# Turns of the RWKV operands placed behind the attention units, and a reordered HGRN2 head on TensorE

## The reference

```
# attention: p = softmax(q.k/8 + c_t - c_s, causal), o = p.v
# RWKV-7:
S = S * w_t + (S a_t) b_t^T + v_t k_t^T
y_t = S r_t
# then group norm of y, plus bonus (sum of r*k*r_k) * v, times a gate
```

```
f = lb + (1 - lb) * sigmoid(f_logit);  k = 1 - f;  b = cumsum(log f) within a chunk
a   = einsum('td,sd,tsd->ts', q, k, exp(b_t - b_s), causal)
o   = a @ v + (q * exp(b)) @ state
state = exp(b_last) * state + (k * exp(b_last - b))^T @ v
# o is divided by its root mean square and multiplied by a weight and silu(gate)
```

## Time and profile before

| | us |
|---|---|
| median of three runs (3396.19 to 3407.8) | 3400.59 |
| the profiled execution | 3394.34 |
| its span | 3392.6 |
| TensorE busy (97%) | 3306.0 |
| VectorE busy (57%) | 1931.4 |
| ScalarE busy (37%) | 1254.7 |

### The profile page before, as it was taken

How to read it: one execution, slowest core, us unless ns; L and a number is a source line. 1 busy time by engine, 2 the same in 40 slices (tenths; PEclk the granted TensorE clock), 3 DMA queues, 4 the chain that set the end, 5 groups by cost and what they waited for, 6 DMA issues and landing times.

```text
span 3392.6 us, 50022 instructions
## 1 busy us (share of the span) xinstructions
PE 3306.0 (97%) x18459; PEld 2704.5 (80%) x18459; DVE 1931.4 (57%) x3749; ACT 1254.7 (37%) x1622; POOL 132.2 (4%) x54
## 2 busy tenths in 40 slices
PE   8998999999899999999999999999999999999998
PEld 6665877878577788888878887888888888888886
DVE  5455456552565544452355999998885444444443
ACT  3333233322455433342343334444544333333332
POOL 0000000000000000000001545000000000000000
PEclk9987999999999999999999999999999999999999
DMA  4110012323222222222332444455556655555542
GB/s 145 56 38 1 4 51 81 99 93 100 86 65 67 80 76 79 80 74 93 100 106 79 148 141 143 156 180 182 185 177 220 228 198 192 198 194 196 198 142 81
DMA packets 145995, 408.03 MB, mean 120 GB/s; under 512 B 11225, under 2 KB 43993, under 8 KB 143585
## 3 DMA queue, kind: packets, MB, share of 16 engines
q1 hardware_dynamic: 73520, 265.85, 25.7%
q10 hardware_dynamic: 72368, 140.68, 11.5%
HBM read 337.28 MB, written 69.21 MB: 120 GB/s over the span
## 4 chain that ended last, share of the span: by engine, by line
PE 87%; DVE 10%; ACT 1%; issue 1%; DMA 1%; ACTq 0%; DVEq 0%; SPq 0%
PE bank L337 24%; PE bank L339 24%; PE bank L338 24%; PE bank L959 2%; PE bank L445 2%; PE bank L957 2%; PE bank L889 1%; ACT arena L1000 1%; PE bank L464 1%; DVE arena L2057 1%; PE bank L503 1%; DVE arena L2020 1%; DVE arena L2021 1%; DVE arena L2023 1%; PE bank L372 1%
## 5 line engine op out<-in xcount | busy, mean ns | idle before, releaser
L337 PE MATMUL bank<-xs,ring_hi 128*128 128x512 f32 x2488 | 990.9, 398 | 19.9 <-DVE xs L1564 9.7
L339 PE MATMUL bank<-xs,ring_lo 128*128 128x512 f32 x2488 | 971.8, 391 | 0.0
L338 PE MATMUL bank<-xs,ring_hi 128*128 128x512 f32 x2488 | 971.3, 390 | 0.0
L1000 ACT ACTIVATE arena<-bank 128x512 f32<-128x512 f32 (+4 forms) x584 | 392.1, 706 | 1013.1 <-PE bank L339 726.8
L1000 ACT ACTIVATE ring_hi<-ring 128x1024 fp32r<-128x1024 f32 x503 | 532.4, 1061 | 621.4 <-DMA ring<-weights 425.3
L1557 DVE TENSOR_TENSOR ring_lo<-ring,ring_hi 128x1024 fp32r<-128x1024 f32 x246 | 300.2, 1224 | 519.5 <-ACT ring_hi L1000 484.0
L337 PEld LDWEIGHTS bank<-xs,ring_hi 128*128 128x128 f32 x2488 | 468.8, 188 | 127.9 <-issue 14.4
L339 PEld LDWEIGHTS bank<-xs,ring_lo 128*128 128x128 f32 x2488 | 468.3, 188 | 100.9
L338 PEld LDWEIGHTS bank<-xs,ring_hi 128*128 128x128 f32 x2488 | 469.2, 189 | 97.1 <-issue 3.4
L2070 DVE TENSOR_TENSOR ring_lo<-ring,ring_hi 128x1024 fp32r<-128x1024 f32 x206 | 252.6, 1226 | 387.3 <-ACT ring_hi L1000 387.2
L337 PE MATMUL bank<-gw,ring_hi 128*128 128x512 f32 x1024 | 398.5, 389 | 0.7 <-ACT arena L1000 0.7
(11 more groups left out here) (285 smaller groups left out, 3408.4 us busy)
## 6 DMA issues: line engine op xcount, KB each, us to landing
ring<-weights SPq DMA_DIRECT2D x503, 512.0 KB, 3.6
hidden<-arena ACTq DMA_DIRECT2D x128, 256.0 KB, 4.1
gates<-arena ACTq DMA_DIRECT2D x16, 2048.0 KB, 6.6
arena<-hidden ACTq DMA_DIRECT2D x16, 2048.0 KB, 10.3
arena<-gates ACTq DMA_DIRECT2D x16, 2048.0 KB, 16.9
xres<-x_t ACTq DMA_DIRECT2D x4, 512.0 KB, 6.5
out_t<-arena SPq DMA_DIRECT2D x4, 512.0 KB, 3.0
arena<-ret_decay ACTq DMA_DIRECT2D x1, 1024.0 KB, 5.9
```

Source lines behind the costliest of these rows:

```text
L337: pe.matmul(out_, wh, x[0], start=start, stop=False, skip_group_check=True)
L338: pe.matmul(out_, wh, x[1], start=False, stop=False, skip_group_check=True)
L339: return pe.matmul(out_, wl, x[0], start=False, stop=stop, skip_group_check=True)
L1000: return act.activation(out_, in_, f, **kw)
```

## The change

**RWKV turns.** The six turns of TA and TB leave `rw_prepare`, with ScalarE's copies and the two semaphores. The late stage now turns TA, TB, TK and RV of all four pairs, sixteen turns in that order. All counts of `rw_act` and `rw_pe` behind it grow by 6.

**HGRN2 head.** The turned keys wait for a semaphore of their own, `hg_keys`, given after KD. The products by chunk stand in front of the scores. The outputs are issued from inside the fourth dense block, in front of its last chunk. ScalarE's square stands in front of Silu. VectorE's mask of the scores waits for the fourth step of `hg_pe` and the state chain for the third.

```diff
-                if u in (19, 20, 23, 24, 27, 28):
-                    i, g0 = (u - 19) % 4, (u - 19) // 4
-                    pe.wait_ge(rw_dve, 2 * g0 + 2)
-                    if 2 * g0 + i:
-                        pe.wait_ge(tok_out, 2 * g0 + i)
-                    for g in range(TT):
-                        tr = pe.transpose(bank[1][:, g * P:(g + 1) * P], tile((TA, TB)[i] + g0)[:, g * P:(g + 1) * P], cc("ident"))
-                    tr.then_inc(tok_ready, 1)
                 if u in (17, 21, 25, 29):
                     pe.wait_ge(rw_dve, 2 * m + 1)
-                    if m:
-                        pe.wait_ge(tok_out, 2 * m)
...
             pe.wait_ge(rw_dve, 8)
-            pe.wait_ge(tok_out, 2 * (NPAIR - 1))
-            late = [(TA, 3), (TB, 3)] + [(TK, m) for m in range(NPAIR)] + [(RV, m) for m in range(NPAIR)]
-            for j, (src, m) in enumerate(late):
+            for i, (src, _) in enumerate(((TA, MA), (TB, MB), (TK, MK), (RV, MV))):
+                for m in range(NPAIR):
+                    j = 4 * i + m
...
                     if r == 0:
-                        pe.wait_ge(rw_act, 30)
+                        pe.wait_ge(rw_act, 36)
...
-                pe.wait_ge(hg_dve, h * 6 + 4)
+                pe.wait_ge(hg_keys, h + 1)
                 for g in range(TT):
                     tr = pe.transpose(bank[5][:, g * P:(g + 1) * P], tile(H_["KD"])[:, g * P:(g + 1) * P], cc("ident"))
                 tr.then_inc(hg_pe, 1)
-                for g in range(TT):
-                    cols = slice(g * P, (g + 1) * P)
-                    mm = pe.matmul(bank[6][:, cols], tile(H_["KD"])[:, cols], tile(H_["QD"])[:, cols],
-                                   start=True, stop=True, skip_group_check=True)
-                mm.then_inc(hg_pe, 1)
                 pe.wait_ge(hg_act, h * 6 + 4)
...
-                product(q + 3, [(B_HG + 3, KD)], XS, h, 4, 4)
-                pe.wait_ge(hg_dve, h * 6 + 6)
+                pe.wait_ge(hg_dve, h * 6 + 4)
...
+                def outputs(k):
+
+                    if k != KD - 1:
+                        return
+                    pe.wait_ge(hg_dve, h * 6 + 6)
...
+                product(q + 3, [(B_HG + 3, KD)], XS, h, 4, 4, outputs)
...
-                if u in (20, 21, 24, 25, 28, 29):
-                    i, g0 = (u - 20) % 4, (u - 20) // 4
-                    act.wait_ge(tok_ready, 2 * g0 + i + 1)
-                    A(tile((MA, MB)[i] + g0), bank[1][:, :], ACT.Copy).then_inc(tok_out, 1)
...
+                act.wait_ge(hg_pe, h * 6 + 5)
+                A(tile(H_["SQ"]), bank[7][:, :], ACT.Square).then_inc(hg_act, 1)
                 act.wait_ge(block_used, h * 4 + B_HG + 4)
-
                 act.wait_ge(hg_dve, h * 6 + 1)
                 A(tile(H_["G"]), bank[(q + 3) % NBANK][:, :], ACT.Silu).then_inc(evac, 1)
                 dense(B_HG + 6, h, 4)
-                act.wait_ge(hg_pe, h * 6 + 5)
-                A(tile(H_["SQ"]), bank[7][:, :], ACT.Square).then_inc(hg_act, 1)
...
-                st.go(TTN(tile(H_["KD"]), tile(H_["K"]), tile(H_["EM"]), ALU.mult))
+                TTN(tile(H_["KD"]), tile(H_["K"]), tile(H_["EM"]), ALU.mult).then_inc(hg_keys, 1)
...
+                ve.wait_ge(hg_pe, h * 6 + 4)
+                TTN(v4(tile(H_["AM"])), v4(bank[6][:, :]), mask4("incl_T"), ALU.mult).then_inc(hg_dve, 1)
                 ve.wait_ge(hg_pe, h * 6 + 3)
-                TTN(v4(tile(H_["AM"])), v4(bank[6][:, :]), mask4("incl_T"), ALU.mult).then_inc(hg_dve, 1)
-                ve.wait_ge(hg_pe, h * 6 + 4)
```

More of the change, by code:

```diff
@@ L826, in _ @@
                 mm.then_inc(hg_pe, 1)
[L827 to L828 removed]
+                pe.wait_ge(hg_dve, h * 6 + 4)
                 for g in range(TT):
                     cols = slice(g * P, (g + 1) * P)
[L831 to L837 removed]
+                    mm = pe.matmul(bank[6][:, cols], tile(H_["KD"])[:, cols], tile(H_["QD"])[:, cols],
+                                   start=True, stop=True, skip_group_check=True)
+                mm.then_inc(hg_pe, 1)
+                def outputs(k):
+                    if k != KD - 1:
+                        return
+                    pe.wait_ge(hg_dve, h * 6 + 6)
+                    for g in range(TT):
+                        cols = slice(g * P, (g + 1) * P)
+                        pe.matmul(bank[7][:, cols], v4(tile(H_["IT"]))[:, g, :], tile(H_["AM"])[:, cols],
+                                  start=True, stop=False, skip_group_check=True)
+                        for c in (2 * g, 2 * g + 1):
+                            if c:
+                                mm = pe.matmul(bank[7][:, c * C:(c + 1) * C], H_["S"](c), tile(H_["QD"])[:, c * C:(c + 1) * C],
+                                               start=False, stop=(c % 2 == 1), skip_group_check=True)
+                    mm.then_inc(hg_pe, 1)
+                product(q + 3, [(B_HG + 3, KD)], XS, h, 4, 4, outputs)
                 pe.wait_ge(hg_act, h * 6 + 5)
@@ L1140, in _ @@
             pair_copy(NPAIR - 1)
-            late = [(MA, 3), (MB, 3)] + [(MK, m) for m in range(NPAIR)] + [(MV, m) for m in range(NPAIR)]
-            for j, (dst, m) in enumerate(late):
-                act.wait_ge(rw_pe, 20 + j + 1)
-                A(tile(dst + m), bank[j % 2][:, :], ACT.Copy).then_inc(rw_act, 1)
+            for i, dst in enumerate((MA, MB, MK, MV)):
+                for m in range(NPAIR):
+                    act.wait_ge(rw_pe, 20 + 4 * i + m + 1)
+                    A(tile(dst + m), bank[(4 * i + m) % 2][:, :], ACT.Copy).then_inc(rw_act, 1)
             for r in range(2):
-                pb = 30 + RW_PE * r
+                pb = 36 + RW_PE * r
                 for lev in range(5):
@@ L1165, in _ @@
                 A(XS[k][0], tile(OF + k), ACT.Copy).then_inc(hi_ready, 1)
-            bp = 30 + RW_PE * 2 + 22
-            ba = 30 + RW_ACT * 2
+            bp = 36 + RW_PE * 2 + 22
+            ba = 36 + RW_ACT * 2
             for m in range(NPAIR):
```

28 lines of the change are left out of this document (11 added, 17 removed).

## The result

| | before | after |
|---|---|---|
| median of 7 runs | 3396.19 us (3391.18 to 3410.45) | 3366.29 us (3362.43 to 3383.43) |
| profiled execution | 3394.34 us | 3383.43 us |
| mean granted clock of it | 0.984 | 0.985 |

The ratio is 0.992 (95% interval 0.9895 to 0.9945). The medians lie 30 us apart, where 15.6 were forecast.

What follows compares the result with a forecast made beforehand. TensorE was taken as the bound (87% of the last-ending chain). From 3394.3 us, 9.5 for the loop and 6.2 for eight heads left 3378.6; with the median 6.2 above the profiled run, 3385 us, range 3371 to 3399.

Steps and rivals of the forecast that it cites:

- part 1: Attention loop: six turn groups move behind it; 11.2 us removed, 4.2 added, 7.0 at the old clock, 9.5 taken.
- The sign that was to decide: Granted clock from 250 to 300 us: 0.65 to 0.8 for the forecast, over 0.9 for the first rival.
- The bonus product's wait for VectorE: Attention loop: wait for VectorE's first step of the pair, costed at nothing; shows if TensorE outruns VectorE by a unit.
- the clock term: Attention loop: clock effect of removed waits, between 11 us lost and 18.5 gained for part 1; 9.5 gained taken.
- The upper end: Attention loop at full clock, bounded by VectorE: 66.7 us become 44, 22.7 less, 18.5 net of late groups.
- the third rival: Clock wakes later without the dense transposes: part 1 loses its gain, heads give 6, median about 3396; chance 0.10.
- Part 2: Recurrence head: chunk products before scores, key transposes waiting only for decayed keys; gain 0.2 us a head.
- Part 3: Recurrence head: outputs ahead of the fourth block's last chunk, sum of squares at T + 8.3; gain 0.57 us a head.
- The clock stays up: Attention loop mostly at 2.4 GHz, VectorE the bound: part 1 gives 15 to 18 us, median 3377; chance 0.27.
- Outputs wait for the state chain: Recurrence heads: part 3 gains nothing, parts 1 and 2 together 9 us, median 3391; chance 0.13.
- The slower case: Late stage and first chunk products at low clock: 27 us more, less 6, median 3422; chance 0.05.
- The base: Whole kernel: median before taken as 3400.59 us, 6.2 us above the profiled execution, added to the sum.

Runs made afterwards that it cites:

- e12: The changed kernel once more, unchanged: 3364.46 us, ratio 0.9923; its profile is nearer the median.
- e1: Kernel before with only the six RWKV turns moved behind the loop, heads unchanged: 3375.15 us, ratio 0.9929.
- e3: Kernel before, all turns left in the loop, ScalarE copying each turned tile one unit earlier in its queue: 3368.33 us, ratio 0.9914.
- e5: Changed kernel plus eight matmuls of 128 x 512 without use in unit 13: 3367.25 us, ratio 0.9918.
- e7: e3's edit (turns in the loop, earlier copies) with the recurrence heads of the changed kernel: 3361.15 us, ratio 0.9899.
- e8: e9 with the eight matmuls of e5 added: 3358.32 us, ratio 0.9888.
- e9: e7 with head turns moved into the third block, scores into the fourth, state chain ahead of the mask: 3352.26 us, ratio 0.9881.
- e6: Kernel before plus the same eight matmuls without use in unit 13: 3395.44 us, ratio 0.9998.
- e10: Kernel before with ScalarE copying both tiles where it copied the first, so only the turn of TB waits: 3385.19 us, ratio 0.9983.
- e11: Kernel before with the first copy a unit earlier, the second unchanged, so only the bonus product waits: 3385.69 us, ratio 0.9987.
- e4: e1 with TensorE still waiting at the old places for ScalarE copies of the same size, without use: 3398.55 us, ratio 1.0012.
- e2: Kernel before with only the recurrence head's reordering, turns unchanged: 3386.73 us, ratio 0.9972.

## Why the prediction was right or wrong, point by point

**The steps that held.** The waits behind VectorE's decayed queries, ahead of the sum of squares, and behind ScalarE's copies in the loop left as said. Sixteen late groups took 11.25 us for the 11.4 forecast; the first stood at 303.94 us in the profile after, for 304 forecast. That agreement is luck: the execution profiled was the slowest of seven, with a low stretch that reached to 271 us. In it part 1 gives 324.93 - 315.19 = 9.7 us, the forecast term. In e12 it gives 324.93 - 298.35 = 26.6 us. The sign that was to decide, the clock from 250 to 300 us, would have misled in the same way. It reads 0.79 in the profile after, inside the forecast's 0.65 to 0.8, but through one fall that began before 250 us and not through falls as before; in e12 it reads 1.00. The bonus product's wait for VectorE, costed at nothing, came: three times in e12, 1.5 us in all.

**The step that failed** is the choice of the clock term: 9.5 us, "nearer to 7.0, since the clock was just as low where TensorE had no wait (215 to 250 us...)". Part 1 alone measured 19 us by the medians and 24 by the ratio (17 to 32, e1). The row was right and the inference was not. It shows how long one fall lasts, with TensorE busy all the while; it says nothing about what starts the next ones. The kernel before falls once near 221 us without a wait, as every kernel here does, and then three times within 3 us of a wait behind a copy. I weighed the first as evidence against the others. The right question was: if these waits go, which fall has a reason left? None behind 250 us, as e3, e5, e7, e8, e9 and e12 show.

The arithmetic of it, from the earlier trace rows and the e12 rows: from 215 to 311 us the kernel before spent 24 us (0.66 over 35) and 41 us (0.66 over 61) at 1.2 GHz, some 65 us; e12 spent 10 (0.85 over 35). Work that runs at half speed for 55 us less saves up to 27 us. From its own side: the way to the first late turn is 317.71 - 287.10 = 30.6 us shorter, and six groups at 0.68 us (4.0) come back behind it.

**The upper end** of that term was too low too, 18.5 against 26.6 us. Reckoning VectorE as the next limit was right, as its 33.68 busy of 35 us show. But I began at 250.98 us, and of the 7.9 us by which the way to the first late turn shrank beyond my 22.7, 4.0 came earlier (bonus product at 239.30 for 243.32), because how long the first low stretch lasts varies; 1.2 came behind the last bonus product (8.5 us before, 7.3 in e12), a part that I had held fixed; the other 2.7 lie between.

**The Trainium skill** ("TensorE: Matmul & The Clock Gate", section on what is actually happening), with its "the default state is throttled, and activity releases the throttle", was weighed both ways in the prediction. Its good side came true: idleness out, clock up. Its bad side, that the dense transposes were needed, didn't behind 271 us: e1, e5 and e12 have none of the six groups in the loop and stay at 1.00 behind the first stretch. For the first stretch itself it stays open (see the third rival). The eight added matmuls of e5 and e6, more activity in the plainest sense, changed nothing; in these runs it was the missing idleness that counted.

**The heads.** Forecast 0.77 us a head, measured 0.63 (30.30 to 29.67), so 5.0 instead of 6.2 us. Part 2 gave 0.30 for 0.2. Part 3 gave 0.34 for 0.57: the outputs came at T + 5.18 instead of T + 5.05, since the chain ended at T + 5.12, and outputs and the last three matmuls took 3.35 us, not 3.25. ScalarE's slack of 3.37 us fell to 0.52, for 0.6 reckoned, and nothing of its later root reached TensorE. The drain that the Trainium skill ("ScalarE: Activation LUTs", section on what a table load costs) puts beside each load didn't show again: the load at 1026.49 took 1.28 us, and the next instruction started at 1027.78.

**The rivals.** "The clock stays up", given 0.27, was the right mechanism; its 17 us for part 1 stand against 19 to 24 in e1 and 26.6 in the rows of e12, so its median of 3377 us was 11 us too slow as well. "Outputs wait for the state chain" came to some 0.3 us a head, not 0.57. The clock did not stand low in the chunk products. That it wakes later is neither shown nor excluded. In e12 it didn't (up at 233 us, 1.00 from there on). But in the profiles of the five kernels without the six groups in the loop the first low stretch ended at 233, 236, 245, 267 (e1) and 271 us (after), and in those of the nine kernels with them between 231 and 249. No run tests whether the groups end it; if they do, it is one more reason why e3 (3368.33) is faster than e1 (3375.15) by more than the 4 us of late groups. The slower case was not seen in any run.

**The base.** 3400.59 us was the median of three runs. In the 7, 23, 17 and 23 runs beside the result and the experiments it was 3396.19, 3394.41, 3393.91 and 3391.19 us. With a base of 3396 my sum would have read 3380.5, still 14 us too slow; the base is not the reason for the miss, but 4 of the 19 us between 3385 and 3366.29 are its. The range moved with it would have begun at 3366.6, right at the measured median; that closeness would have been luck, since the clock term was wrong all the same.

**What stays open:** why the clock falls near 220 us, where TensorE is busy without a gap, and what decides whether that stretch lasts 10 us (e3, e12), 24 (before), 48 (e1) or 51 (the profile after). Between the two profiles of the changed kernel it makes 17 of 19 us (first chunk product at 315.19 and 298.35 us, executions of 3383.43 and 3364.43 us), and by the mean clocks most of the spread from 3362 to 3383 us. What stands there is the same in all fourteen traces: 32 products of 2 columns (218.57 to 222.66 us in the kernel before, fall at 221.6). The eight added matmuls show only that a few larger ones among them don't prevent it; a run without these products is missing.

## What to carry to other kernels

Price a wait of the bounding engine by the clock that follows it, and ask of each fall of the clock what stands right ahead of it; a low stretch that has another reason is no evidence against that. To get rid of a wait behind a copy, first let the copying engine do it earlier in its queue (e3, two lines, 26 us by the medians) before moving the work itself behind the loop (e1, 19 us by the medians, with 4 us of new work in sight). When a program has a few runs with another mean clock, look at the clocks of all runs before reading one profile as the kernel's.

## What the hardware showed that was not expected

- Six waits of 6.6 us in all cost the kernel before some 26 us (e3). The first two falls behind them lasted 20 and 17 us there (255.7 to 276.2, 283.0 to 300.1 us).
- Place matters: in the heads of the kernel before, waits of 0.98 us (the eight of the earlier trace rows) among 128 x 512 matmuls left the clock at 1.00, as this row shows, of three heads; in the attention loop waits of 0.95 us brought it down. Small products around the wait are not enough for that: between the 64 x 64 products behind the late turns a wait of 1.48 us, of the kernel before too, left the clock at 1.00. What about the place decides is not shown.

```profile
1000.00:1100.00 100.00, 94.31 (x497) 1.00 0.22 68
```

```profile
326.00:332.00 6.00, 4.52 (x203) 1.00 0.02 5
```

```profile
329.49 0.51 PE L345 MATMUL bank<-ring_hi 128*128 128x512 f32 x1 [1.48 <-DVE arena L1727]
```

- Half as many waits still left the loop, from 250 to 300 us, at a mean clock of 0.73 (e10, e11). With all six it was 0.63 (before), 0.66 (e6), 0.72 (e4) and 0.73 (e2), so half as many are hardly better by this measure. With none it was 1.00 (e3, e5, e7, e8, e9, e12), but for the two executions whose first low stretch reached to 267 and 271 us (e1 0.83, after 0.79).
- In e11 the clock fell inside the wait. TensorE, by single microseconds ahead of the bonus product at 258.23 us; it is idle for the first:

```profile
257.00:258.00 1.00, 0.00 (x0) 0.86 0.00 0
258.00:259.00 1.00, 0.77 (x1) 0.50 0.00 0
```
